# One product for both parts of the attention probabilities, and a PSUM bank per head

## What is computed

```
s = (einsum('bqhc,bkc->bhqk', q_lat, c) + einsum('bqhr,bkr->bhqk', q_rope, kr)) * ATTN_SCALE
s = where(kpos <= qpos, s, -inf)
p = softmax(s, axis=-1)
o_lat = einsum('bhqk,bkc->bqhc', p, c)
o = einsum('blhc,chv->blhv', o_lat, w_uv)
h = h + o.reshape(...) @ w_o
```

## Time and profile before

| | |
|---|---|
| median of 3 runs | 734.32 us (734.07 to 734.36) |
| the profiled execution | 735.66 us |
| its span, first to last instruction | 733.9 us |
| granted clock of TensorE, mean | 0.999 |
| TensorE, matmuls (PE) | 726.2 us, 99% |
| TensorE, weight loads (PEld) | 711.1 us, 97% |
| VectorE (DVE) | 307.2 us, 42% |
| ScalarE (ACT) | 410.0 us, 56% |
| GpSimd (POOL) | 535.7 us, 73% |

### The profile page before, as it was taken

How to read it: one execution, slowest core, us unless ns; L and a number is a source line. 1 busy time by engine, 2 the same in 40 slices (tenths; PEclk the granted TensorE clock), 3 DMA queues, 4 the chain that set the end, 5 groups by cost and what they waited for, 6 DMA issues and landing times.

```text
span 733.9 us, 16735 instructions
## 1 busy us (share of the span) xinstructions
PE 726.2 (99%) x6275; PEld 711.1 (97%) x6275; DVE 307.2 (42%) x774; ACT 410.0 (56%) x749; POOL 535.7 (73%) x254
## 2 busy tenths in 40 slices
PE   8999999999999999999999999999999999999997
PEld 8999999999999999999999888799999999999997
DVE  5446976223233232222478776853232333321101
ACT  6887555456444444555677666564564444444543
POOL 4896678878888788898868121249878887888892
PEclk9999999999999999999999999999999999999999
DMA  7764454656767755566566799316546555555641
GB/s 244 263 202 144 142 176 158 204 188 199 242 231 237 232 192 184 185 198 204 182 248 210 251 342 353 148 59 211 190 144 201 177 191 175 187 184 181 205 161 60
DMA packets 44587, 144.68 MB, mean 197 GB/s; under 512 B 5635, under 2 KB 6019, under 8 KB 44275
## 3 DMA queue, kind: packets, MB, share of 16 engines
q1 hardware_dynamic: 44210, 143.47, 58.5%
q0 software_dynamic: 176, 0.44, 0.2%
q10 hardware_dynamic: 144, 0.02, 0.0%
HBM read 142.42 MB, written 1.48 MB: 196 GB/s over the span
## 4 chain that ended last, share of the span: by engine, by line
PE 97%; DMA 1%; ACT 1%; DVE 0%; issue 0%; SPq 0%; ACTq 0%
PE ps L1404 29%; PE ps L1405 29%; PE ps L1406 29%; PE ps L1812 1%; PE ps L1788 1%; PE ps L1481 1%; PE ps L1473 1%; DMA raw<-w_stream 1%; PE ps L1474 1%; PE ps L1732 1%; PE ps L1541 1%; PE ps L1450 1%; PE ps L1659 0%; PE ps L1792 0%; PE ps L1718 0%; PE ps L1720 0%
## 5 line engine op out<-in xcount | busy, mean ns | idle before, releaser
L427 POOL TENSOR_TENSOR wlo<-raw,whi 128x1024 fp32r<-128x1024 f32 x221 | 527.2, 2410 | 182.3 <-ACT whi L500 182.2
L1404 PE MATMUL ps<-xhi,whi 128*128 128x264 f32 x1000 | 286.2, 286 | 0.0
L1405 PE MATMUL ps<-xlo,whi 128*128 128x264 f32 x1000 | 283.3, 283 | 0.0
L1406 PE MATMUL ps<-xhi,wlo 128*128 128x264 f32 x1000 | 283.3, 283 | 0.0
L500 ACT ACTIVATE whi<-raw 128x1024 fp32r<-128x1024 f32 x221 | 232.8, 1055 | 50.8 <-PE ps L1406 48.5
L1405 PEld LDWEIGHTS ps<-xlo,whi 128*128 128x128 f32 x1000 | 188.5, 189 | 0.1
L1404 PEld LDWEIGHTS ps<-xhi,whi 128*128 128x128 f32 x1000 | 188.3, 188 | 0.2
L1406 PEld LDWEIGHTS ps<-xhi,wlo 128*128 128x128 f32 x1000 | 187.5, 188 | 0.0
L1404 PE MATMUL ps<-ahi,whi 128*128 128x264 f32 x352 | 100.0, 284 | 0.0
L1406 PE MATMUL ps<-ahi,wlo 128*128 128x264 f32 x352 | 99.9, 284 | 0.0
L1405 PE MATMUL ps<-alo,whi 128*128 128x264 f32 x352 | 99.9, 284 | 0.0
(11 more groups left out here) (281 smaller groups left out, 1158.6 us busy)
## 6 DMA issues: line engine op xcount, KB each, us to landing
raw<-w_stream SPq DMA_DIRECT2D x221, 512.0 KB, 3.3
pg<-pages SPq DMA_DIRECT2D x64, 288.0 KB, 4.3
pg<-w_ukT SPq DMA_DIRECT2D x1, 2048.0 KB, 9.3
pg<-w_uv SPq DMA_DIRECT2D x1, 2048.0 KB, 10.3
h<-xT SPq DMA_DIRECT2D x4, 264.0 KB, 5.2
raw<-w_stream SPq DMA_DIRECT2D x4, 256.0 KB, 6.6
wsraw<-wsT SPq DMA_DIRECT2D x1, 512.0 KB, 5.7
bsb<-bs SPq DMA_DIRECT2D x1, 512.0 KB, 5.7
```

Source lines behind the costliest of these rows:

```text
L427: pool.tensor_tensor(wlo[:, c % RING, :], raw[:, c % RING, :], whi[:, c % RING, :].bitcast(F32), ALU.subtract).then_inc(lo_ready, 1)
L1404: pe.matmul(out, whi_, mhi, start=start, stop=False)
L1405: pe.matmul(out, whi_, mlo, start=False, stop=False)
L1406: return pe.matmul(out, wlo_, mhi, start=False, stop=stop)
```

## The change

- `attend` writes each head into a bank of its own. Banks 2, 3 and 0 go round: `score_bank(p, e)` and `head_bank(p, e)` give the three places of scores and results, and the second half of a result's bank holds what the low part of the probabilities adds in the high-by-low passes. High and low parts of the probabilities lie side by side (`ptboth`), so that one product of 512 columns replaces two of 256, and one of 256 replaces two of 128: a head is four products.
- ScalarE and VectorE take the result a head at a time. VectorE subtracts (256 columns) and then adds the second half of the bank (256 columns). `scores(p)` waits, ahead of its second head, until the first head of the pair before has been read.
- The scores come out negated (the scale of the queries changes its sign), so that minima take the place of maxima, the exponential takes a scale of -1, and the negation is dropped. The exponential of the wider part goes first and waits for its own minimum alone.
- On ScalarE the result's two copies go ahead of the next weight slab's split, but in pair 7. On VectorE `differences()` goes behind the result of pair 5.

```
+        def score_bank(p, e):
+            return (2, 3, 0)[(p + e) % 3]
+
+        def head_bank(p, e):
+            return (2, 3, 0)[(p + 2 + e) % 3]
...
             def exponentials(p, e):
-                act.wait_ge(nm_done, 2 * p + e + 1)
-                for part, (lo, hi_) in enumerate(((0, P), (P, 3 * P))):
-                    act.activation(pr[:, e, lo:hi_], pr[:, e, lo:hi_], ACT.Exp, bias=nmh[:, e, part:part + 1],
+                for x, (part, lo, hi_) in enumerate(((1, P, 3 * P), (0, 0, P))):
+                    act.wait_ge(min_done, 2 * (2 * p + e) + x + 1)
+                    act.activation(pr[:, e, lo:hi_], pr[:, e, lo:hi_], ACT.Exp, bias=mnh[:, e, part:part + 1], scale=-1.0,
                                    accum_out=rsh[:, e, part:part + 1]).then_inc(exp_done, 1)
...
-            def heads_high(p):
-                act.wait_ge(pv_done, p + 1)
-                act.activation(ohi[:, 2 * p:2 * p + 2, 0:NP_], key_views(0), ACT.Copy).then_inc(ohi_done, 1)
+            def head_high(p, e):
+                act.wait_ge(pv_done, 2 * p + e + 1)
+                act.activation(ohi[:, 2 * p + e, 0:NP_], ps[:, head_bank(p, e), 0:NP_], ACT.Copy).then_inc(ohi_done, 1)
...
                 if p < PAIRS - 1:
                     keys_high(p + 1)
+                else:
+                    split(PR_S + p + AHEAD)
                 if MID[p] is not None:
                     sample_turned(MID[p])
-                split(PR_S + p + AHEAD)
-                heads_high(p)
+                head_high(p, 0)
+                head_high(p, 1)
+                if p < PAIRS - 1:
+                    split(PR_S + p + AHEAD)
                 if p == JOIN:
                     act.wait_ge(dd_done, 2)
                     act.activation(ww, dd, ACT.Exp).then_inc(ww_done, 1)
...
-                dve.wait_ge(max_done, 2 * (2 * p + e) + 2)
-                dve.tensor_scalar(nmh[:, e, :], mxh[:, e, :], -1.0, None, ALU.mult).then_inc(nm_done, 1)
...
-            def heads_low(p):
-                dve.wait_ge(ohi_done, p + 1)
-                lo_of(olo[:, 2 * p:2 * p + 2, 0:NP_], key_views(0), ohi[:, 2 * p:2 * p + 2, 0:NP_]).then_inc(olo_done, 1)
+            def head_low(p, e):
+                dve.wait_ge(ohi_done, 2 * p + e + 1)
+                out, low = ps[:, head_bank(p, e), :], olo[:, 2 * p + e, 0:NP_]
+                lo_of(low, out[:, 0:NP_], ohi[:, 2 * p + e, 0:NP_]).then_inc(omain_done, 1)
+                dve.wait_ge(omain_done, 2 * p + e + 1)
+                dve.tensor_tensor(low, out[:, NP_:2 * NP_], low.bitcast(F32), ALU.add).then_inc(olo_done, 1)
...
                 if p < PAIRS - 1:
                     keys_low(p + 1)
-                if p == JOIN:
-                    differences()
                 if p == JOIN + 1:
...
-                heads_low(p)
+                head_low(p, 0)
+                head_low(p, 1)
+                if p == JOIN:
+                    differences()
...
                 for e in range(2):
-                    both = ps[:, 2 + e, :].rearrange("p (h k) -> p h k", k=P)[:, 0:4:3]
+                    if p and e:
+                        pe.wait_ge(olo_done, 2 * p - 1)
+                    bank = ps[:, score_bank(p, e), :]
+                    both = bank.rearrange("p (h k) -> p h k", k=P)[:, 0:4:3]
...
                 for e in range(2):
                     pe.wait_ge(ptlo_done, 2 * p + e + 1)
                     w = slice(e * P, e * P + P)
-                    passes(ps[:, 0, e * NP_:(e + 1) * NP_], vhi[:, 0, w], vlo[:, 0, w], pthi[:, e, 0:NP_],
-                           ptlo[:, e, 0:NP_], True, False)
-                    last = passes(ps[:, 0, e * NP_ + P:(e + 1) * NP_], vhi[:, 1, w], vlo[:, 1, w],
-                                  pthi[:, e, NP_:3 * P], ptlo[:, e, NP_:3 * P], False, True)
-                last.then_inc(pv_done, 1)
+                    out = ps[:, head_bank(p, e), :]
+                    both = out.rearrange("p (l k) -> p l k", l=2)
+                    pe.matmul(both, vhi[:, 0, w], ptboth[:, :, e, 0:NP_], start=True, stop=False)
+                    pe.matmul(out[:, 0:NP_], vlo[:, 0, w], pthi[:, e, 0:NP_], start=False, stop=False)
+                    pe.matmul(both[:, :, P:NP_], vhi[:, 1, w], ptboth[:, :, e, NP_:3 * P], start=False, stop=False)
+                    pe.matmul(out[:, P:NP_], vlo[:, 1, w], pthi[:, e, NP_:3 * P], start=False, stop=True).then_inc(pv_done, 1)
```

More of the change, by code:

```diff
@@ L188, in build @@
         cqhi, cqlo = (x[:, 0:3 * T].rearrange("p (a b) -> p a b", a=3) for x in (flat_hi, flat_lo))
-        kboth = flat_hi[:, 0:4 * NP_].rearrange("p (l a k) -> p l a k", l=2, a=2)
+        kboth = flat_lo[:, 0:4 * NP_].rearrange("p (l a k) -> p l a k", l=2, a=2)
         khi, klo = kboth[:, 0], kboth[:, 1]
-        vhi, vlo = (halves(flat_lo[:, x * 2 * NP_:(x + 1) * 2 * NP_]) for x in range(2))
-        pthi, ptlo = (halves(x[:, 4 * NP_:4 * NP_ + 6 * P]) for x in (flat_hi, flat_lo))
+        vhi, vlo = (halves(flat_lo[:, x * 2 * NP_:(x + 1) * 2 * NP_]) for x in (2, 3))
+        ptboth = flat_hi[:, 0:12 * P].rearrange("p (l a k) -> p l a k", l=2, a=2)
+        pthi, ptlo = ptboth[:, 0], ptboth[:, 1]
         half = [slice(0, P), slice(P, T)]
@@ L450, in _ @@
             for at in (0, 2 * P):
-                pool.affine_select(out=mask[:, at:at + P], in_=mask[:, at:at + P], compare_op=ALU.is_ge, fill=NEG,
+                pool.affine_select(out=mask[:, at:at + P], in_=mask[:, at:at + P], compare_op=ALU.is_ge, fill=-NEG,
                                    base=0, pattern=[[-1, P]], channel_multiplier=1).then_inc(const_done, 1)
             for sign in (1, -1):
-                pool.affine_select(out=off_diag[:], in_=off_diag[:], compare_op=ALU.is_ge, fill=NEG, base=0,
+                pool.affine_select(out=off_diag[:], in_=off_diag[:], compare_op=ALU.is_ge, fill=-NEG, base=0,
                                    pattern=[[-sign, NS], [0, H]], channel_multiplier=sign).then_inc(const_done, 1)
@@ L1277, in maximum @@
                     dve.wait_ge(pt_done, 2 * p + e - 1)
[L1278 to L1281 removed]
+                dve.tensor_tensor(pr[:, e, 0:P], ps[:, score_bank(p, e), 3 * P:4 * P], mask[:, 0:P], ALU.add).then_inc(scl_done, 1)
+                dve.tensor_tensor_reduce(out=pr[:, e, P:3 * P], in0=ps[:, score_bank(p, e), P:3 * P], in1=mask[:, P:3 * P], scale=1.0,
+                                         scalar=-NEG, op0=ALU.add, op1=ALU.min,
+                                         accum_out=mnh[:, e, 1:2]).then_inc(min_done, 1)
                 dve.wait_ge(scl_done, 2 * p + e + 1)
[L1283 to L1286 removed]
+                dve.tensor_tensor_reduce(out=pr[:, e, 0:P], in0=ps[:, score_bank(p, e), 0:P], in1=pr[:, e, 0:P], scale=1.0, scalar=-NEG,
+                                         op0=ALU.add, op1=ALU.min, accum_out=mnh[:, e, 0:1]).then_inc(min_done, 1)
             def normal(p, e):
@@ L1720, in scores @@
                     pe.matmul(both, qrb[:, 2 * p + e, qs], krboth[:, :, 0:P], start=False, stop=True)
-                    out = ps[:, 2 + e, P:3 * P]
+                    out = bank[:, P:3 * P]
                     qs = slice(P, 2 * P)
@@ L1731, in turn @@
                 for b in range(3):
-                    last = pe.transpose(ps[:, 2 + e, b * P:b * P + P], pr[:, e, b * P:b * P + P], ident[:])
+                    last = pe.transpose(ps[:, score_bank(p, e), b * P:b * P + P], pr[:, e, b * P:b * P + P], ident[:])
                 last.then_inc(pt_done, 1)
@@ L1899, in first_of_wo @@
             def first_of_wo(b0, b1):
-                main(*STAGES["wo"], KS, headed, ready=lambda b: pe.wait_ge(olo_done, b // 2 + 1), part=(b0, b1),
+                main(*STAGES["wo"], KS, headed, ready=lambda b: pe.wait_ge(olo_done, b + 1), part=(b0, b1),
                      bank_free=False, bank=WO_BANK)
```

38 lines of the change are left out of this document (16 added, 22 removed).

## The result

The changed kernel took **735.47 us** (median of 19 runs), the kernel before 734.22 us (19 runs on the same chip); the ratio is 1.0033, with an interval of 1.0023 to 1.0043. The forecast was 735.2 us. The median lies 0.3 us from it and 1.25 us, or 0.17%, above the kernel before, but the ratio, which is that of the mean times (736.70 to 734.31 us), says more: slower by 0.33%, over the 0.2% that I had called no change. The two differ because the changed kernel's runs fall into two groups. Eleven took 734.59 to 735.53 us with a granted clock of 0.998 to 1.0 in the mean; one took 737.8 us at 0.995, and six 739.3 to 739.8 us at 0.991 to 0.993. The nineteenth took 4059.96 us at a clock of 1.0, which no trace here explains; it is in neither group and not in the mean, and without it the median is 735.4 us. The kernel before has no second group, its slowest run being 735.29 us.

The account below looks back on a forecast made before the run. TensorE, busy 99% of the span, was taken as the bound, with keys and weights having no slack. Terms -0.12 - 0.24 - 0.24 - 0.2 + 1.70 = +0.90 us on 734.32 gave 735.2 us, range 733.2 to 737.2.

Parts of the forecast that it names:

- a head's saving: Attend's products on TensorE: four in place of six save 0.12 us a head, 1.9 us over sixteen heads if nothing waits.
- The price of the wide product: Attend's first product of 512 columns: 0.23 us to the next start, 0.31 behind a transpose; bounds 0.21 and 0.24.
- this sign of being right: Sign in attend's trace that the forecast holds: a first product of about 0.23 us to the next start.
- that rival: Attend's products of 512 columns take 0.131 us, the skill page's figure: 734.7 us; chance 0.04.
- The full saving: Rival for attend: no wait bites, all saved products count, 1.92 + 0.2 us less, 732.2 us; chance 0.08.
- The keys: Scores after pairs 1, 2 and 4: keys are there at A + 1.44 (A: first attend product), so these pairs save nothing.
- The join: Sample tokens at pair 5: differences() behind four VectorE operations delay the weights, TensorE idles, pair 5 ends 1.70 us later.
- The rival in which narrow operations are dear: VectorE's operations on a head's result take 0.69 us each, not 0.43: +3.2 us, 737.5 us; chance 0.18.
- a chain that TensorE meets only in pair 7: Dropped negation and earlier wider exponential shorten a chain that matters only in pair 7: -0.2 us, between 0 and -0.23.
- Pair 6's zero: Pair 6: room for its keys against a VectorE copy ahead of its result, taken as 0, between -0.24 and +0.2 us.
- the signs and masks: Negated scores' signs and masks: the same operations as before, so they cost nothing.
- slower by over 0.2%: Whole-kernel case: the dear narrow operations plus 0.05 of the forecast's upper end; chance 0.23.

Follow-up runs that it names:

- e9: e1 with the six products per head of the kernel before in attend, in place of four; 734.57 us, ratio 1.0007.
- e7: The kernel before with the low part of the next keys written in two halves, each score head waiting for its own; 734.03 us, ratio 0.9996.
- e4: Changed kernel with differences() ahead of pair 5's result, weights() between its halves, their exponential ahead of the slab's split, keys in halves; 736.28 us, ratio 1.0031.
- e6: The kernel before with the negated scores alone: minima, scale of -1, wider exponential first, no negation; 734.28 us, ratio 0.9998.
- e1: Changed kernel with VectorE's differences() put back ahead of pair 5's result; 733.66 us, ratio 0.9996.
- e8: Changed kernel with the clearing of the weights' tile done four times, to lengthen TensorE's idle stretch at the join; 739.87 us, ratio 1.0054.
- e3: Changed kernel with its products of both probability parts cut into halves, six products a head again; 740.08 us, ratio 1.0060.
- e2: The kernel before with only differences() moved behind the result of pair 5; 735.78 us, ratio 1.0019.
- e5: e4 with pair 5's slab split on ScalarE moved behind the sample tokens' output, so GpSimd starts later; 733.25 us, ratio 0.9984.

## Why the prediction held, and where it did not

**The products**: a head's saving was sized right, 0.12 us forecast against 0.10 and 0.15 measured (0.72 to 0.62 and to 0.57, 424.39 to 424.90 and 0.06). The price of the wide product was right behind a transpose, 0.31 us forecast and 0.32 measured, but not elsewhere: 0.28 us in place of 0.23, outside the bounds of 0.21 and 0.24, so that this sign of being right did not come. It did no harm, since the two products that it replaces in a second head also take 0.28 us there (425.72 to 426.00), and not 0.24. The Trainium skill's page TensorE: Matmul & The Clock Gate, section "Back-to-back issue gap", states about 131 ns for 512 columns in a stream; the trace, with 0.28 to 0.32 us, does not agree, and that rival falls. The full saving falls with e9: 0.91 us of 1.9.

**The keys** in pairs 1, 2 and 4 came out to the hundredth: A + 1.44 before and after. e7 and e4 together show the mechanism from both sides: earlier keys bring 0.02 to 0.04 us a pair with six products and 0.18 us with four.

**The join** is the mechanism forecast, a little smaller. The sum had pair 5 end 1.70 us later; the turn of the weights went from A + 4.60 to A + 6.13, 1.53 us later. The mis-sized term is `differences()`. The four operations ahead of them were right: they began at A + 1.22 (forecast 1.27), and the differences at A + 2.86 (2.89). But these then took 1.57 us (468.17 to 469.74) where I had taken 1.76 over from the earlier trace rows. All of the 0.19 us lies in the first two of them, the clearing (0.09 us to the next start, 0.21 before) and the copy (0.28, 0.35 before). The exponential, 0.27, and the weights, 1.31, were as forecast. The rival in which narrow operations are dear falls: 0.41 to 0.43 us each, not 0.69.

**Pair 0** is the step that failed: "a chain that TensorE meets only in pair 7". TensorE met it in pair 0 too, where the low probabilities hang on the exponentials; I had used that wait, to cut the products' saving and had not asked whether the shorter chain removes it. The changed kernel's rows show it removed:

```profile
411.82 0.56 DVE L883 TENSOR_TENSOR xhi<-ps,xhi 128x384 fp32r<-128x384 f32 x1 [0.48 <-ACT xhi L805]
...
412.56 0.45 PE L1761 MATMUL ps<-xhi,xlo 128*128 128x512 f32 x1
```

The low part ends at 412.38, 0.18 us before the second head. e6 gives the chain 0.16 us of pair 0, the products have the other 0.21. Pair 3 gained less than forecast: the products are worth 0.21 us there (e9 against e1), and 0.05 us go the other way with the negated scores alone (11.85 us in e6, 11.80 before).

**Pairs 6 and 7** held, but for where a wait falls. Pair 6's zero was a balance of a saving and of a VectorE copy that stands ahead of its result, and so it came: attend(6) to scores(7) is 0.18 us shorter (1.22 us, 1.40 before), and the second head of scores(7) waits about 0.19 us, which the table counts to pair 7. Pair 7 itself has 0.22 us from the products (attend(7) to `w_o` 1.11 us, 1.33 before) and some 0.24 us from ScalarE's copy, for which TensorE no longer waits: -0.46 by -0.44. The new wait, VectorE and TensorE:

```profile
478.86 0.42 DVE L1393 COPY pg<-ps 128x256 f32<-128x256 f32 x1
...
479.64 0.42 DVE L1315 TENSOR_TENSOR olo<-ps,olo 128x256 fp32r<-128x256 f32 x1
...
479.92 0.28 PE L1741 MATMUL ps<-krboth,qrb 128*128 128x256 f32 x1
...
480.12 0.38 PE L1734 MATMUL ps<-xlo,ohi 128*128 128x256 f32 x1
```

The addition ends at 480.06, and 480.12 is 0.20 us behind the product before, in place of 0.12, the next start another 0.10 us late. In e6, which has no such wait, pair 7 keeps its 0.26 us.

**What was not forecast at all** is that an idle stretch costs more than its length. The sum of the terms was 0.90 us, and the first group is 0.89 us slower (735.11 - 734.22). That these agree to a hundredth is luck: by the traces only 0.51 us of it lie in the stretch, the join having cost less and pair 0 gained more than forecast. Another 0.17 us lie in the tail, where the prediction had put the signs and masks at nothing and e6 shows 0.15 us for them; the last 0.2 us can't be placed, since executions differ by more ahead of the stretch (scores(0) starts at 403.1 to 404.7 us in the traces of this study). The seven runs with a lower clock, and the one of 4059.96 us, raise the median by another 0.36 us; the seven raise the ratio to 1.0033. With them, the case "slower by over 0.2%", with a chance of 0.23, is nearer to the ratio than "no change" with 0.67.

## What to carry to other kernels

Where one engine is full, write down for each of its inputs by how much it is early; a saving is worth no more than the smallest of these, and the next one (here keys at 0, then the second score head's bank, at 0.27 us by the forecast) takes over as soon as the first is mended. Before a chain is moved behind other work, even on an engine that is busy for 62.5 of 89.5 us, ask what hangs on its last instruction and by how much that was early: here the move cost 1.5 us, more than all the products gave (0.9 us). And look at what then runs beside the moved step on the engine that shares its ports, and count a new idle stretch on TensorE as a risk to its clock, not only at its own length.

## What the runs showed of the hardware

- **The clock falls behind a stretch in which TensorE stood still, in some executions of the same kernel and not in others.** Two traces show the fall itself: e8's above, behind a wait of 2.43 us, and e3's, where the granted clock is 1.00 up to 473 us, behind a wait of 1.63 us that ended at 471.63, then 0.57 and 0.50, and 1.00 again from 484 us. The other executions are known by their times and mean clocks alone. With the changed kernel's wait of 1.7 us seven of eighteen runs are 2.7 to 4.7 us over its first group's median, with e3's 1.63 us four of six, with e8's 2.43 us six of eight, with e1's 0.3 us none of eleven; none of eleven against seven of eighteen would come by chance about once in fifty times. The wait of 1.5 us in e2 brought it in none of eleven, while e4, with a wait of the same length at the sample latents, has clocks of 0.994 to 0.997 in six of eleven; that these fell behind that wait is not shown, and what tells the two apart is open.
- **A tiny VectorE operation that reads and writes SBUF can take as long as what is left of GpSimd's running one.** The masked weights, with both inputs in SBUF, took 1.91 us in e4, 0.98 in e9 and 0.75 in e1, each time ending 0.14 to 0.15 us behind GpSimd's operation, and 0.27 us in the nine other traces. The kernel before has it as well, on a line without weight: its negation of two maxima, 128 x 2 elements with one input, took 0.51 us in place of 0.17 at 428.87, ending 0.04 us behind GpSimd's operation of 426.95 + 2.39.
- **Most products of 128 columns cost hardly less than one of 256.** In e9 the second and third of the short products take 0.11 us to the next start, the first 0.06, the long ones 0.12; the loads of their weights start 0.11 to 0.13 us apart for either (423.39, 423.52, 423.63, 423.75 and 423.86 us). So most of a head's saving comes from the merged short product (three in 0.28 us before, two in 0.18 now) and little from the long one (0.45 to 0.44 in a first head, 0.40 in either kernel in a second).
- **A wait of TensorE holds the load of the weights too, and its cost is the load's delay.** In a dense row a load starts 0.11 us ahead of its product (426.15 and 426.26 in the changed kernel's pair 1), and the next product follows 0.12 us later. Behind e5's wait the load is 0.20 us late, its product 0.12 us (425.43) and the next product 0.19 us; behind the one in the changed kernel's pair 7 it is 0.19, 0.08 (480.12) and 0.18 us.
